# The order of VectorE's work in each turn of the second expert stage

## What is computed

```python
    def chunk(xc):
        ...
        fv, fi = lax.top_k(cand, PEER_TOPK)
        idx = jnp.take_along_axis(cidx, fi, axis=-1)
        g = jax.nn.softmax(fv, axis=-1)
        u = u_tab[idx]
        a = jax.nn.gelu(jnp.einsum('chkd,cd->chk', u, xc).astype(jnp.float32), approximate=False)
        vv = v_tab[idx]
        return jnp.einsum('chk,chkd->cd', (g * a).astype(vv.dtype), vv)
```

## Time and profile before

| | |
|---|---|
| median of 3 runs | 2846.78 us |
| lowest and highest of them | 2843.03 and 2854.58 us |
| the profiled execution's own time | 2853.3 us |
| its span, first to last instruction | 2851.5 us |
| PE busy over the span | 2591.1 us, 91% |
| DVE busy over the span | 1743.9 us, 61% |
| DMA bytes over the span | 504.04 MB, 177 GB/s |

### The profile page before, as it was taken

One profiled execution on the slowest core, in us unless ns is written; L12 is line 12 of the kernel. 1 busy time (PEld: TensorE's weight loads), 2 busy tenths in 40 slices (PEclk: granted clock), 3 DMA queues, 4 the chain that ended last, 5 costly groups with the idle time before them and its releaser, 6 DMA issues. The chain is left out here.

```text
span 2851.5 us, 48163 instructions
## 1 busy us (share of the span) xinstructions
PE 2591.1 (91%) x18276; PEld 2293.2 (80%) x18276; DVE 1743.9 (61%) x3004; ACT 1076.6 (38%) x1745; POOL 1035.0 (36%) x686
## 2 busy tenths in 40 slices
PE   6999989999999998599999999699799888999997
PEld 4766768899999998598998889567699765887875
DVE  1354339996998996667777777628466654333015
ACT  3366333344343333133233333445334454333233
POOL 2622333466333334412222221233444432444442
PEclk9999999999999999799999999899899989999998
DMA  3211222455888899989999998224722011323331
GB/s 132 96 60 45 89 89 81 124 144 175 301 313 321 302 347 328 330 282 314 325 311 316 306 318 289 89 82 166 241 59 52 17 30 59 96 96 96 104 96 52
DMA packets 210211, 504.04 MB, mean 177 GB/s; under 512 B 59392, under 2 KB 108672, under 8 KB 208768
## 3 DMA queue, kind: packets, MB, share of 16 engines
q1 hardware_dynamic: 173184, 367.52, 39.5%
q0 software_dynamic: 36864, 134.23, 13.1%
HBM read 434.57 MB, written 67.11 MB: 176 GB/s over the span
## 5 line engine op out<-in xcount | busy, mean ns | idle before, releaser
L152 ACT ACTIVATE weights_high<-weights_raw 128x1024 fp32r<-128x1024 f32 x433 | 458.7, 1060 | 1312.3 <-PE psum L260 1312.1
L160 POOL TENSOR_TENSOR weights_low<-weights_raw,weights_high 128x1024 fp32r<-128x1024 f32 x219 | 550.8, 2515 | 833.4 <-ACT weights_high L152 833.2
L258 PE MATMUL psum<-expert_in_high,weights_high 128*128 128x384 f32 (+1 forms) x1152 | 407.9, 354 | 35.8 <-ACT expert_activation L1162 13.1
L258 PE MATMUL psum<-coefficients_high,weights_high 128*128 128x384 f32 x1024 | 352.9, 345 | 58.1 <-DVE weights_low L160 42.5
L259 PE MATMUL psum<-expert_in_low,weights_high 128*128 128x384 f32 (+1 forms) x1152 | 396.9, 345 | 0.0
L260 PE MATMUL psum<-expert_in_high,weights_low 128*128 128x384 f32 (+1 forms) x1152 | 396.5, 344 | 0.0
L260 PE MATMUL psum<-coefficients_high,weights_low 128*128 128x384 f32 x1024 | 346.3, 338 | 0.0
L259 PE MATMUL psum<-coefficients_low,weights_high 128*128 128x384 f32 x1024 | 346.2, 338 | 0.0
L1388 POOL DMA_INDIRECT expert_rows<-in_u_rows,row_numbers x128 | 186.5, 1457 | 303.3 <-DVE row_coefficients L1402 289.1
L1388 POOL DMA_INDIRECT expert_rows<-in_weights,row_numbers x128 | 144.8, 1131 | 417.6 <-DVE s_by_token_then_row_sums L1428 378.4
L160 DVE TENSOR_TENSOR weights_low<-weights_raw,weights_high 128x1024 fp32r<-128x1024 f32 x214 | 261.3, 1221 | 39.4 <-ACT weights_high L152 39.2
(11 more groups left out here) (398 smaller groups left out, 4989.5 us busy)
## 6 DMA issues: line engine op xcount, KB each, us to landing
weights_raw<-in_weights SPq DMA_DIRECT2D x435, 512.0 KB
expert_activations<-expert_activation SPq DMA_DIRECT2D x128, 192.0 KB
coefficient_table<-table_stage SPq DMA_DIRECT2D x8, 3072.0 KB, 13.6
table_group<-coefficient_table SPq DMA_DIRECT2D x128, 192.0 KB
activation_in<-expert_activations SPq DMA_DIRECT2D x128, 192.0 KB
a_and_kk_then_chunks<-scan_vectors SPq DMA_DIRECT2D x8, 768.0 KB, 6.6
scan_vectors<-scan_stage SPq DMA_DIRECT2D x4, 1280.0 KB, 7.1
scan_vectors<-scan_stage SPq DMA_DIRECT2D x4, 1024.0 KB, 6.1
```

The source lines that it names most:

```text
L152: act.activation(d.hi[:, m % SPLIT, :], d.raw[:, m % RAW, :], ACT.Copy).then_inc(d.high, 1)
L160: pool.tensor_tensor(d.lo[:, m % SPLIT, :], d.raw[:, m % RAW, :], d.hi[:, m % SPLIT, :].bitcast(F32), ALU.subtract).then_inc(d.split, 1)
L258: pe.matmul(acc, w[0][:, cols], x[0], start=start, stop=False)
```

## The change

In each turn of the V stage VectorE's steps change places. Before, the next tile's product comes first, then the coefficients' low part, then the weights' low part, then the row sums. Now the weights' low part comes first, then the coefficients' low part, then the next tile's product, and then the row sums. No step is added or removed, and no other engine's program changes.

```diff
                 multiply(0)
                 for n in range(ex.ut):
-                    if n + 1 < ex.ut:
-                        multiply(n + 1)
+                    if n >= SPLIT:
+                        w.low(dve, 0, n - SPLIT, ex.ut)
                     o = n % ex.CR
                     dve.wait_ge(ex.high, n + 1)
                     dve.tensor_tensor(co[1][:, o, :], a_in[:, n % ex.AR, :], co[0][:, o, :].bitcast(F32),
                                       ALU.subtract).then_inc(ex.coef, 1)
-                    if n >= SPLIT:
-                        w.low(dve, 0, n - SPLIT, ex.ut)
+                    if n + 1 < ex.ut:
+                        multiply(n + 1)
                     rows.add_rows(dve, n, ex.ut)
```

## The result

| | |
|---|---|
| median after, 4 runs | 2780.05 us (2777.56 to 2781.86) |
| median before, 4 runs | 2850.68 us (2843.03 to 2857.76) |
| ratio | 0.9752, 95% interval 0.9723 to 0.9782 |

The kernel is 2.5% faster, some 70 us, where 33 were forecast. The time lies 8 us under the low end of the range, 2788: it is the case that had 13%, TensorE as the bound.

The account below looks back on a forecast made before the run. It took the DMA engines as the V stage's next bound: 115 x (4.71 - 4.43) = 32 us, with the end 33; 2853.3 - 33 = 2820, and 6.5 less for the median: 2814 us, range 2788 to 2842.

Parts of the forecast that it names:

- TensorE as the bound: Rival, 13%: in the V stage the queues carry 360 GB/s and all waits go, 64 us won, 2782 us.
- The loop: V stage: a late activations' load for tile n + 1 holds up tile n; two turns before, three after.
- The sum of 4.78 us and L: V stage, new three-turn loop: issue steps, load time, product, row sum and low part; 10.62 us with L 5.84, 3.54 a turn.
- The load's time L: Activations' load, issue to landing: 5.84 us before, 7 to 8.5 expected after; the new loop bears 7.7.
- What bounds it next: the DMA engines: V stage after the change: a turn's bytes at 334 and 364 GB/s need 4.34 us of all engines, above TensorE's 4.15.
- It agrees with 0.91 of 4.71: Check of the V stage's 4.34 us DMA time against the DMA share 0.91 of the mean turn, 4.71 us.
- 4.43: Forecast V-stage turn in us, with the DMA engines at 98%; against 4.71 before, 32 us won over 115 turns.
- The signs: V-stage profile marks: DMA share 0.96 or more if right; well under 0.95 with PE waiting for nothing if TensorE bound.
- my own case: Likeliest case, 62%: DMA engines bound the V stage, 19 to 43 us won, 2804 to 2828 us.
- The low parts: V stage, VectorE's two low parts swapped: costs nothing in the body, wins 0.4 us in the last turn.
- The gathers: Rival "slower", 6%: gathered rows for the V stage's row sums come late; at 15.5 us, 31 us slower, 2878.
- Little is won: Rival, 16%: V-stage load time grows with fuller queues; at 9.3 us the new loop is as slow as the old; 2837 us.

Follow-up runs that it names:

- The two halves of the change: Against the kernel before: only the product moved last, low parts in old order, 2785.9 us; only the low parts swapped, product still first, 2836.3 us.
- the two moves on SP together with the old order: Kernel before, VectorE unchanged, SP issuing activations about one turn earlier and table pieces in front of the weights' load: 2785.2 us, ratio 0.9756.
- the late issue with the new one: Changed kernel with SP issuing the activations behind its weights and table loads, one turn later: 2890.6 us, ratio 1.0135 to the kernel before.
- the first of the two moves alone: Kernel before, VectorE unchanged, SP asking only for the activations about one turn earlier: 2815.3 us, ratio 0.9869.
- both loads early: SP issues activations about one turn earlier and table pieces before the weights' load: 2785.2 us on the kernel before, 2784.95 us with VectorE's new order.

## Why the prediction was wrong

**The loop was right.** The load for the next tile held up this tile's low parts; behind the change it spans three turns, and it stopped binding. The two halves of the change, the two moves on SP together with the old order, and the late issue with the new one came out on its side; the first of the two moves alone missed, since the table stands in the same loop. The sum of 4.78 us and L gave 4.9 to 5.1 us a turn for the late issue; it was 5.09. The load's time L was wrong: I expected 7 to 8.5 us with fuller queues, and the median is 5.6. A single load of 8.6 us, over the 7.7 that the loop bears if every load takes that long, made no wait of PE.

**What failed is the step "What bounds it next: the DMA engines".** I divided each queue's bytes by its share, took 334 and 364 GB/s as what the engines can do, and made a floor of 4.34 us a turn, over TensorE's 4.15. The changed kernel itself moved 358 GB/s with PE busy 459.93 of 460 us, and the runs with extra bytes put the limit near 380 GB/s. The mix's 1.496 MB a turn then take 3.94 us, so TensorE bounds. The check that I gave, "It agrees with 0.91 of 4.71", was none: it multiplies the share back in by which the bytes had been divided. With the same sum and TensorE's 4.15 in place of 4.43 the forecast would have been 2853.3 - 65 = 2788 us for that profile's execution, 2782 for the median. I had written this down as a rival, with the row that spoke for it (390 GB/s in the U stage), and set it aside because "its rate by share is steady over 490 us, and the packets are of another kind". The steady ratio was that of one load on the engines, and with the same packets it rose from 315 GB/s at 0.91 to 358 at 0.98. The signs misled as well: a share of 0.96 or more came, as for my own case, and the one that I had set for TensorE as the bound, a share well under 0.95, did not.

The Trainium skill's limit of about 358 GB/s for a core (DMA: Bandwidth & Descriptors, Specifications) gave an estimated 4.18 us, nearer than my own figure, but it was not the bound: with extra bytes this core moved 383 GB/s. The Trainium skill's fabric ceiling of 435 GB/s (same section) was not reached in any stretch given here.

**The low parts.** In the last turn the change was worth what I said: ScalarE's high part to PE took 3.30 us in the earlier trace rows and takes 1734.32 - 1731.49 = 2.83 us now, 0.47 won for 0.4 forecast.

```profile
1731.49 1.06 ACT L152 ACTIVATE weights_high<-weights_raw 128x1024 fp32r<-128x1024 f32 x1 [2.41 <-PE psum L260]
...
1734.32 0.66 PE L1438 MATMUL psum<-tables,s_by_token_then_row_sums 128*128 128x64 f32 x4 [2.93 <-DVE coefficients_low L1279]
```

In the body I called it nothing, and it was about 7 us in a pair of profiles. With both loads early the order made no difference (4.16 us a turn either way), so the 4.15 us in which TensorE works on the tile before cover it while nothing is late.

**The rivals.** The gathers never came late: no wait for one stands in the list of the changed kernel from turn 4 on. "Little is won" needed loads of 9 us as the rule, and their median was 5.6.

**The rest of the surplus.** The profiled pair gained 63 us in the turns and the medians 70. The second pair of profiles has 71 in the turns: of the two profiles of the old kernel, I worked from the one with the shorter turns. That the sum with TensorE's turn lands within 2 us of the median after is in part luck, since it has a gain of 65 us and the medians moved by 70. How much of the remaining 3 or 4 us behind the stage is the change's stays open.

## What to carry to other kernels

Count the turns from the point that lets a load be issued to the first thing it holds up that the bounding engine needs. One turn more can be had by moving the use back or the issue forward, and here either was worth the same (ratios 0.975 and 0.976). Look at every load on the queue: here the table took the activations' place.

A DMA share near 1 was no proof of a limit here, and bytes divided by the share gave one that was some 10% too low. Add bytes that nobody needs and see where the turn grows.

## What the runs showed of the hardware

The share counts the time of packets, and that time was not the same before and after. SP's queue from 1230 to 1690 us, before and then after (packets, MB, share of 16 engines):

```profile
q1 hardware_dynamic: 41859, 88.95, 58.0%
```

```profile
q1 hardware_dynamic: 47405, 100.79, 60.2%
```

Per packet that is 0.580 x 16 x 460 us / 41859 = 102 ns before and 93.5 ns after, with the same 2.1 KB each; 13% more bytes took 4% more time. The gathers' packets stayed the same (15386 in 33.5%, then 17465 in 37.8%: 160 and 159 ns). Why SP's get shorter no run here shows. With extra bytes the summed share passes 1 (1.02), so it isn't the occupied part of a fixed whole.
